# Attention units one step deeper in order, second norm and first query chunk inside the mixer block, no weight halves in front of expert routing

## The reference, cut to what matters

```
# mixture of experts: routing, then 16 experts of 1024 -> 512 -> 1024
probs = softmax(t @ router_w + router_b)       # best group of 4, then best 2 experts in it
out = sum_e combine[:, e] * ((silu(t @ w_gate[e]) * (t @ w_up[e])) @ w_down[e])
# second block
xn = rmsnorm(h, norm1_g);  proj = xn @ w_in
y_ssm  = s5_branch(u, ...)                     # complex state, scanned over the tokens
y_attn = dsa_branch(q, k, v, qi, ki, wi)       # softmax over the selected keys, 8 heads
merged = sigmoid(g_ssm) * (y_ssm @ w_ssm_up) + sigmoid(g_attn) * (y_attn @ w_attn_up)
h  = h + merged @ w_out
hn = rmsnorm(h, norm2_g)
h  = h + peer_ffn(hn, w_q, k1, k2, u_tab, v_tab)   # q = hn @ w_q first
```

## Time and profile before

| | |
|---|---|
| time, median of 3 | 2379.27 us |
| profiled execution, its own time | 2377.59 us |
| its span | 2375.8 us |
| mean granted TensorE clock | 0.954 |
| busy, share of the span | PE 89%, PEld 74%, DVE 67%, ACT 47%, POOL 28% |
| HBM | 204 GB/s over the span |

### The profile page before, as it was taken

One profiled execution on the slowest core, in us unless ns is written; L12 is line 12 of the kernel. 1 busy time (PEld: TensorE's weight loads), 2 busy tenths in 40 slices (PEclk: granted clock), 3 DMA queues, 4 the chain that ended last, 5 costly groups with the idle time before them and its releaser, 6 DMA issues. The chain is left out here.

```text
span 2375.8 us, 34059 instructions
## 1 busy us (share of the span) xinstructions
PE 2117.2 (89%) x11356; PEld 1749.6 (74%) x11356; DVE 1581.6 (67%) x2562; ACT 1112.7 (47%) x1593; POOL 672.6 (28%) x466
## 2 busy tenths in 40 slices
PE   3987999997995879999968978789899998999997
PEld 3874877775874667777656644788899998888886
DVE  5356788885456368888779641179949997555554
ACT  3353776773341457676530121344454443554454
POOL 4620100003780720000030000669977774000000
PEclk9998999998997979999979989899999999999999
DMA  8864888893484348988722223144444443555554
GB/s 316 311 242 142 303 323 322 325 350 147 169 346 159 124 144 331 344 321 325 303 68 107 89 81 140 54 142 162 165 160 141 141 141 133 186 194 194 193 191 146
DMA packets 76319, 485.54 MB, mean 204 GB/s; under 512 B 9424, under 2 KB 9936, under 8 KB 58320
## 3 DMA queue, kind: packets, MB, share of 16 engines
q1 hardware_dynamic: 75520, 482.88, 56.1%
q10 hardware_dynamic: 720, 1.61, 0.2%
HBM read 483.41 MB, written 1.05 MB: 204 GB/s over the span
## 5 line engine op out<-in xcount | busy, mean ns | idle before, releaser
L1113 DVE TENSOR_TENSOR moe_w_lo<-ring,moe_w_hi 128x1024 fp32r<-128x1024 f32 x376 | 446.9, 1227 | 54.5 <-ACT moe_w_hi L1044 40.3
L1044 ACT ACTIVATE moe_w_hi<-ring 128x1024 fp32r<-128x1024 f32 x376 | 383.8, 1058 | 64.1 <-PE bank L993 33.8
L2688 POOL TENSOR_TENSOR peer_u_lo<-peer_u,peer_u_hi 128x512 fp32r<-128x512 f32 x256 | 347.5, 1370 | 111.7 <-ACT peer_u_hi L2711 110.0
L2651 PE MATMUL bank<-peer_hn_hi,peer_u_hi 128*128 128x256 f32 x1024 | 294.9, 288 | 18.2 <-POOL peer_u_lo L2688 18.2
L2652 PE MATMUL bank<-peer_hn_lo,peer_u_hi 128*128 128x256 f32 x1024 | 286.8, 280 | 0.0
L2653 PE MATMUL bank<-peer_hn_hi,peer_u_lo 128*128 128x256 f32 x1024 | 286.5, 280 | 0.0
L2711 ACT ACTIVATE peer_u_hi<-peer_u 128x512 fp32r<-128x512 f32 x256 | 161.0, 629 | 129.8 <-PE bank L2653 122.3
L225 POOL TENSOR_TENSOR ret_in_w_lo<-ring,ret_in_w_hi 128x1024 fp32r<-128x1024 f32 x48 | 117.1, 2449 | 352.3 <-ACT ret_in_w_hi L219 352.1
L974 PE MATMUL bank<-moe_w_hi,moe_slots_hi 128*128 128x512 f32 x512 | 209.3, 409 | 7.9 <-DVE moe_w_lo L1113 4.2
L2651 PEld LDWEIGHTS bank<-peer_hn_hi,peer_u_hi 128*128 128x128 f32 x1024 | 193.9, 189 | 20.3 <-POOL peer_u_lo L2688 20.0
L976 PE MATMUL bank<-moe_w_hi,moe_slots_lo 128*128 128x512 f32 x512 | 200.8, 392 | 0.0
(11 more groups left out here) (479 smaller groups left out, 4472.4 us busy)
## 6 DMA issues: line engine op xcount, KB each, us to landing
ring<-in_stream SPq DMA_DIRECT2D x135, 2048.0 KB, 8.0
peer_u<-in_peer_u SPq DMA_DIRECT2D x128, 512.0 KB, 3.2
peer_v<-in_peer_v SPq DMA_DIRECT2D x128, 512.0 KB, 3.2
sb_mod_ring<-in_ada_t SPq DMA_DIRECT2D x64, 512.0 KB, 9.0
ret_mod_ring<-in_ada_t SPq DMA_DIRECT2D x32, 512.0 KB, 8.3
s_bz<-in_b_channel SPq DMA_DIRECT2D x4, 512.0 KB, 6.7
ring<-in_stream SPq DMA_DIRECT2D x2, 1024.0 KB, 5.1
moe_room<-in_ln_g SPq DMA_DIRECT2D x3, 512.0 KB, 4.3
```

Of the source, the lines that this page charges most:

```text
L1044: act.activation(w_hi[:, q, :], K.ring[:, at % RING, q * CHUNK // Q:(q + 1) * CHUNK // Q], ACT.Copy).then_inc(hi_done, 1)
L1113: dve.tensor_tensor(w_lo[:, q, :], K.ring[:, at % RING, q * CHUNK // Q:(q + 1) * CHUNK // Q], w_hi[:, q, :].bitcast(F32), ALU.subtract).th ...
L2651: pe.matmul(out, u_hi[:, b, k2, :], h_hi[:, k, :], start=(k == 0), stop=False)
L2688: pool.tensor_tensor(u_lo[:, b, :, :], u[:, i, KD // 2 * half:KD // 2 * (half + 1), :], u_hi[:, b, :, :].bitcast(F32), ALU.subtract).then_ ...
```

## The change

What it does, in the order of the program:

1. Both expert layers: ACT makes two of the four high quarters before the first exponential, moves the diagonal behind that exponential, and makes the other two quarters after the token copies; DVE makes the low quarters after routing and the picking of experts, ahead of `slots_low`, no longer before routing. The chunk's slot is given back there.
2. S5 tables: the absolute value moves from DVE to ACT (`ACT.Abs`, with a wait of ACT on itself). The tables lie in two buffers; the other buffers that reused the one table follow.
3. Attention units: PE issues logits(i+1) where it issued logits(i), and ACT issues the exponentials of unit n+1 ahead of the copy of unit n.
4. The second norm moves into the mixer block, by token halves: `project_out` signals each half row, DVE adds it to x (`add_out`), ACT squares it, and so on to the split high and low parts of the normed input, which ACT and DVE write directly from the transposes. The norm row is fetched during the mixer. ACT makes the four high quarters of the first query chunk ahead of the squares; POOL makes the low ones at the end of its list.
5. The stage between mixer and query product is gone, and `recycle_sems` stands behind the query stage.

```diff
@@ moe_stage @@
+            low((0, 0))
             slots_low(None)
...
-                    if r == 0 and i is None:
-                        dve.wait_ge(lo_done, Q)
-                        dve.sem_inc(K.chunk_used, 1)
...
                 act.wait_ge(K.landed[n0 % RING], 16 * (n0 // RING + 1))
-                for q in range(Q): ... (all four high quarters)
-                gate.scalar_diagonal(act)
+                first_high((0, 1))
                 act.wait_ge(exp_ready, 1)
                 act.activation(ex[:], pr[:], ACT.Exp).then_inc(exp_made, 1)
+                gate.scalar_diagonal(act)
+                act.wait_ge(exp_ready, 2)
+                act.activation(col[:, 5, :], col[:, 4, :], ACT.Exp).then_inc(exp_made, 1)
                 for n in range(4):
                     take_h(n)
-                act.wait_ge(exp_ready, 2)
-                act.activation(col[:, 5, :], col[:, 4, :], ACT.Exp).then_inc(exp_made, 1)
+                first_high((2, 3))
                 gate.scalar_take(act)
...
                 gate.vector(dve)
-                for q in range(Q): ... (four low quarters on DVE)
                 route(dve, c)
@@ second_mixer_stage @@
             sp:
+            fetch_chunks(sp, K, START["w_out2"])
+            sp.wait_ge(rotated, 4)
+            sp.dma_start(norm_row[:], K.A["norm2_g"].to_broadcast([P, D])).then_inc(norm_in, 16)
             fetch_chunks(sp, K, next_start("w_out2") + RING)
             pool, at the end:
+            queries.low(pool, queries.n0, True)
             pe:
             for i in range(len(units) + 2):
-                if 2 <= i < len(units):
-                    logits(i)
+                if 1 <= i < len(units) - 1:
+                    logits(i + 1)
...
-                if tt == 1:
-                    last.then_inc(K.chunk_used, 1)
+                last.then_inc(K.chunk_used if tt == 1 else out_made, 1)
...
+            for tt in range(TT):
+                turn_normed(tt)
             act:
-                act.wait_ge(frac_made, 2 * b + 2)
+                act.wait_ge(frac_made, b + 1)
+                act.activation(tab(first, last, 0), tab(first, last, 1), ACT.Abs).then_inc(abs_made, 1)
+                act.wait_ge(abs_made, b + 1)
...
+            exponentials(0)
+            for n in range(len(units)):
+                if n + 1 < len(units):
+                    exponentials(n + 1)
+                take_turned(n)
...
+            queries.high(act, queries.n0, True)
+            square(0)
+            square(1)
+            deviation(0)
+            square(2)
+            square(3)
+            deviation(1)
+            for n in range(2 * TT):
+                high_normed(n)
             dve:
-                dve.scalar_tensor_tensor(scratch, at, -1.0, at, ALU.mult, ALU.max).then_inc(frac_made, 1)
...
+            add_out(0)
+            half_square(0)
+            add_out(1)
+            dve.wait_ge(x_added, 2)
+            dve.wait_ge(norm_in, 16)
+            normed(0)
+            add_out(2)
+            half_square(1)
+            add_out(3)
+            dve.wait_ge(x_added, 4)
+            normed(1)
+            for n in range(2 * TT):
+                low_normed(n)
@@ program @@
-                S = Second(K, second)
-                rms_norm_turn_stage(K, "norm1", "norm1_g", load=S.load, room=K.mod)
-                second_mixer_stage(K, S)
-            K.recycle_sems()
-            rms_norm_turn_stage(K, "norm2", "norm2_g", before=add_banks(K))
...
-            peer_query_stage(K, scores, h_hi, h_lo)
+                queries = SplitProducts(K, second, "peer_wq", START["peer_wq"], (h_hi, h_lo), x_done=True)
...
+                    second_mixer_stage(K, S, queries)
+                scores = scores_scope.enter_context(nc.sbuf_tensor("peer_scores", [P, TT, 2048], F32, side="right"))
+                peer_query_stage(K, S, queries, scores)
+            K.recycle_sems()
```

More of the change, by code:

```diff
@@ L1324, in _, with first_high @@
             def _(act):
+                def first_high(quarters):
+                    for q in quarters:
+                        act.activation(w_hi[:, q, :], K.ring[:, n0 % RING, q * CHUNK // Q:(q + 1) * CHUNK // Q],
+                                       ACT.Copy).then_inc(hi_done, 1)
                 act.wait_ge(K.landed[n0 % RING], 16 * (n0 // RING + 1))
-                for q in range(Q):
-                    act.activation(w_hi[:, q, :], K.ring[:, n0 % RING, q * CHUNK // Q:(q + 1) * CHUNK // Q],
-                                   ACT.Copy).then_inc(hi_done, 1)
-                gate.scalar_diagonal(act)
+                first_high((0, 1))
                 def take_h(n):
@@ L2128, in project_out, with turn_normed @@
                     last = pe.matmul(K.bank[:, 2 * tt + dh, :], K.hT[:, k, own(tt)], w[:, k, :], start=(k == 0), stop=(k == KD - 1))
-                if tt == 1:
-                    last.then_inc(K.chunk_used, 1)
+                last.then_inc(K.chunk_used if tt == 1 else out_made, 1)
+            def turn_normed(tt):
+                for half in range(2):
+                    pe.wait_ge(hn_ready, 2 * tt + half + 1)
+                    for k in range(4 * half, 4 * half + 4):
+                        last = pe.transpose(K.bank[:, 4 + 2 * tt + half, k % 4 * P:(k % 4 + 1) * P], hn[:, tt, k * P:(k + 1) * P],
+                                            K.ident)
+                    last.then_inc(hn_turned, 1)
             attn_up(0, 0)
@@ L2245, in _, with exponentials @@
                 take_gate(8 + tt, n_last, 3, ACT.Sigmoid)
-            for n, (tt, j) in enumerate(units):
+            def exponentials(n):
+                tt, j = units[n]
                 act.wait_ge(max_ready, n + 1)
@@ L2500, with peer_query_stage @@
 V_SLOTS = 3
-def peer_query_stage(K, scores, h_hi, h_lo):
+def peer_query_stage(K, S, products, scores):
     nc = K.nc
@@ L2509, in peer_query_stage @@
     with ExitStack() as stage, nc.Block() as block:
-        qT = stage.enter_context(nc.sbuf_tensor("peer_qT", [P, 2 * PK_HEADS, T], F32))
-        products = SplitProducts(K, stage, "peer_wq", n_wq, (h_hi, h_lo))
+        qT = S.first_tables[:].rearrange("p (h t) -> p h t", t=T)
         @block.sync
@@ L2537, in _ @@
         def _(pool):
-            for j in range(4):
+            for j in range(1, 4):
                 products.low(pool, n_wq + j, True)
@@ L2542, in _ @@
         def _(act):
-            products.high_x(act)
-            products.high(act, n_wq, True)
             for j in range(4):
@@ L2555, in _ @@
         def _(dve):
-            products.low_x(dve)
             for j in range(4):
```

108 lines of the change are left out of this document (80 added, 28 removed).

## The result

The changed kernel took 2347.02 us, the median of 4 executions (2343.74 to 2348.44); the kernel before took 2379.03 us beside it (2376.43 to 2382.80). The ratio is 0.9862, with a 95% interval of 0.9845 to 0.9880: 32.0 us faster (28.5 to 36.9 by the interval), where 32.7 were predicted. A later series gave 2345.18 against 2382.56 (ratio 0.9843, 0.9830 to 0.9857), 37.4 us. The profiled execution of after took 2348.18 us, span 2346.5, mean granted clock 0.951; PE is busy 90% of it.

A forecast was written before the change was run, and what follows sets the result against it. PE sets the pace in dense stretches; the gains were sought where it lacks work. Terms 3.9 + 4.5 + 9 + 15.3 = 32.7 us took the median 2379.27 to 2346.6, with 2337 to 2354 to hold 8 in 10.

The forecast's parts named there:

- Routing, 3.9: Expert routing, both layers: earlier exponential and gate matmuls, less contention on low quarters, gain 3.9 us; bounds 1.5 and 7.4.
- DVE's `slots_low` would be late next: Expert routing: DVE, now carrying 4.63 us of low quarters, arrives late next; 0.6 us late in the second layer.
- The walk: Step-by-step timing of the expert routing: 2.7 - 0.4 us gained in the first layer, 2.7 - 1.1 in the second.
- Absolute values, 4.5: S5 tables: 3.7 us of DVE time reaching PE plus 0.8 for the slow stretch, gain 4.5; bounds 2.5 and 6.7.
- no PE wait over 3 us: Sign of being right at PE's swap waiting for `rotate` in S5: its 5.39 us wait shrinks to about 1.7.
- Units, 9: Attention units: logits one round earlier shorten the long rounds, gain 9 us; bounds 3 and 13.
- full-clock walk: Attention units at full clock: long rounds lose 26.97 - 16.2 = 10.8 us, the other rounds nothing.
- rival of the held chain: Attention units: DVE's hand-over to PE and ACT stays the bound, part gives 3 us, total 2352.6; chance 0.13.
- Norm, 15.3: Second norm inside the mixer block: gap 23.1 to 7.3 us, less 1.3 recycling, plus 0.8 query chunk; gain 15.3.
- full-clock rival: Fewer idle gaps keep PE at 2.4 GHz in routing, units and norm: 43 us gained, 2336; chance 0.17.
- the slower one: Expert and PEER stages: denser PE work lowers granted clock to 0.97, costing 41 us, 2388; chance 0.02.

The follow-up runs named there:

- e1: The kernel before with only the new order of the expert routing, both expert layers: 2375.69 us against 2379.91, ratio 0.9981.
- e8: The changed kernel with the first query chunk's high and low quarters made behind the mixer block, as before: 2349.46 us, ratio 0.9871 to the kernel before.
- e5: The kernel before with only PE's part of the new unit order, logits of unit i+1 issued earlier: 2368.64 us against 2379.31, ratio 0.9954.
- e9: The changed kernel run again unchanged, as base of a later series: 2345.18 us against 2382.56 for the kernel before, ratio 0.9843.
- e11: The changed kernel with 16 and 8 unread transposes filling PE's pauses in the norm: 2343.66 us, ratio 0.9837 to the kernel before.
- e3: The kernel before with only the deeper order of the attention units, both PE's and ACT's part: 2369.14 us, ratio 0.9956.
- e7: The changed kernel with POOL's scaling of x held back until DVE made the first chunk's four low quarters: 2345.74 us, ratio 0.9851 to the kernel before.
- e6: The kernel before with only ACT's part of the new unit order, exponentials of unit n+1 ahead of unit n's copy: 2379.93 us, ratio 1.0003.
- e10: The changed kernel with each `ssm_up` product split over two rounds and DVE taking it one unit later: 2340.14 us, ratio 0.9818 to the kernel before.
- e12: The changed kernel with split `ssm_up`, filled norm pauses, POOL's scaling held back and ACT's old unit order: 2340.12 us, ratio 0.9817 to the kernel before.

## Why the prediction was right

The places, the waits and the way were right, and the total to 0.7 us. That it was so near is luck: one term was 4 us too small, and a loss of 3.1 that nobody foresaw cancelled most of it. The second series, with 37.4, shows how little the 0.7 means.

- **Routing, 3.9:** 3.7 + 1.4 in the routings, less 0.8 given back in the rest of the first layer and 0.3 in that of the second (303.0 us for 302.6 from its first expert product to the writing back): 4.0; alone 4.2. The exponential came 4.2 us earlier as worked out, the low quarters beside POOL cost 1.6 more (2.0 forecast). That DVE's `slots_low` would be late next was wrong for after, where PE isn't idle before L974 in either layer; it came true in the second layer of e1 and e8, by 0.4 and 0.7 us. What was late in after was the gathering at 1.2 GHz: PE is busy with it 2.0 and 2.3 us longer than before, and from its start to its end it takes 1.2 and 2.3 more (a pause in the middle of the first was shorter). The walk left that out, and it charged 0.4 and 1.1 for a contention that this hid: errors of opposite sign.
- **Absolute values, 4.5:** 4.7 by stage, 4.3 alone. But PE's wait at the swap did not shrink from 5.39 to 1.7. Everything ahead of it, PE's products included, follows DVE's tiles, so PE arrived earlier as well and waited as long. The sign "no PE wait over 3 us" was wrong, the sum right.
- **Units, 9:** 13.0 by stage. This is the mis-sized term. The full-clock walk gave 10.8, I took off 1.8 for slow stretches and set 13 as the bound. Logits alone, at the full clock throughout, show what was missing: the three long rounds shrink to 14.9 us where 16.2 were taken (5.0, 5.0 and 4.8), the two short ones lose 1.2 and the end of the stretch, behind the last round, 2.1, both put at nothing; in all 15.5. The slow stretches that remain take 1.6 to 3.3 back where there are any. Over the stretch the mean clock is 1.00 in three of the seven profiles with the logits early and `ssm_up` whole (e5, e9, e11), with pauses of 1.3 to 2.4 us left, and 0.91 to 0.95 in the four others (after, e3, e7, e8); in the five with the old order it is 0.80 to 0.86. The Trainium skill, TensorE: Matmul & The Clock Gate, section "A second HAM failure mode: psum-queue depth-cycling", tells of another kernel whose clock swings with such pauses. The traces here go both ways, and what decides it no run shows. The rival of the held chain falls: exponentials in front of the copy cost nothing (e6), and the part gave 13.0, not 3.
- **Norm, 15.3:** 16.7 - 1.6 = 15.1; alone 14.4. The gap was 6.6 for 7.3. The query stage with the recycling behind it is 1.6 longer, where 1.3 - 0.8 = 0.5 was forecast: the query products end 0.3 us earlier on the mean (49.6 for 49.9), and PE's wait in front of the first PEER product is 1.9 longer (8.5 for 6.6), in the profiles of before and of after:

```profile
1563.61 0.58 PE L2651 MATMUL bank<-peer_hn_hi,peer_u_hi 128*128 128x256 f32 x1 [6.27 <-POOL peer_u_lo L2688]
```

```profile
1530.45 0.58 PE L2756 MATMUL bank<-peer_hn_hi,peer_u_hi 128*128 128x256 f32 x1 [9.10 <-POOL peer_u_lo L2793]
```

  The squares stood behind the four high quarters (until 1442.1), but the chunk had landed, and it cost nothing.
- **Not foreseen, -3.1 in PEER.** The group of ACT's high parts over the first 200 us of that stage (group, busy time, mean ns, idle time by releaser), of the norm part alone and then of after:

```profile
L2806 ACT ACTIVATE peer_u_hi<-peer_u 128x512 fp32r<-128x512 f32 x127 | 79.9, 629 | 34.2 <-PE bank L2748 33.1 <-DMA peer_u<-in_peer_u 0.7
```

```profile
L2816 ACT ACTIVATE peer_u_hi<-peer_u 128x512 fp32r<-128x512 f32 x125 | 78.6, 630 | 38.2 <-PE bank L2758 32.5 <-issue 3.9
```

Once in about 8.6 us, which is one turn of ACT's loop over three tiles, ACT starts late for no reason the profile names. POOL's low part follows it, and PE's product follows that: PE's starts from the 300th to the 1500th of this stage's products span 157.6 to 158.2 us in the seven profiles with the late starts and 155.4 to 155.9 in the others.

```profile
1606.87 0.39 ACT L2809 ACTIVATE H<-bank 128x256 f32 x1 [0.86 <-PE bank L2758]
1607.45 1.36 ACT L2816 ACTIVATE peer_u_hi<-peer_u 128x512 fp32r<-128x512 f32 x2 [0.19 <-issue]
```

The 3.9 us of "issue" stand in all seven profiles of kernels that hold the whole change (after twice, and e7, e8, e10, e11 and e12, each with small edits), and in none of the seven others (before, the parts and the half parts). The loop's code is the same in all. No single part brings it. That it hangs on where the loop lies in ACT's program is my guess; no run tested it.

So the sum is 4.0 + 4.7 + 13.0 + 15.1 - 3.1 = 33.7 us. The full-clock rival (43 us) was right about the units only; the slower one (clock of the dense stages under 1.00) did not appear: the window 300 to 400 stands at 1.00 again, and so do those of 50 us from 250 to 400 us into PEER.

## What to carry to other kernels

Where an in-order engine has a long product in front of a short one that starts another engine's chain, issue the short one first; and then spread the long product, so that it fills the waits that remain: 13 us came from reordering TensorE's list alone, and 4 more from the split, for which one product of VectorE moved along. A stage pace read from one pair of profiles can be off by more than a part of the change is worth: stages that nothing edits show how much. Contention, slower low parts and a late engine cost only what the last arriver lets through.

## What the runs showed of the hardware

- An engine's loop can cost more or less from one program to another with the same body: 3.9 us of "issue" in 200 us on ACT in seven profiles and none in seven, and 3.1 us on the stage's mean. The cause is open.
- Pauses of 2.10 and 1.68 us behind a dense stretch were followed by matmuls at 1.2 GHz; with transposes nobody reads in their place (e11, e12) the clock stayed at 2.4, and the next stage was 2 us shorter. In the unit loop pauses of 1.3 to 2.4 us were followed by 1.2 GHz in one execution of after (mean clock 0.95) and not in the other (1.00).
- DVE and POOL slow each other: 1.16 to 1.56 us for a subtraction of 128x1024, 0.69 to 1.19 for a multiplication of 128x256 (means, e7 and after).
- An absolute value on ACT between sines needed no table load: the timeline of ACT shows five of them (0.41 to 1.06 us) and no load between 1215 and 1260 in after.
